# Eight gather slots and eight kept weight chunks in a two-layer encoder with gathered experts

## What is computed

```
h = h + mixer_ab(rmsnorm(h), ...)          # layer 0: stick-breaking attention heads + short gated convolution
h = h + peer(rmsnorm(h), w_q[0], keys[0], u[0], v[0])
h = h + mixer_conformer(rmsnorm(h), ...)   # layer 1: pw1 (1024x2048), GLU, 31-tap conv, layernorm, SiLU, pw2
h = h + peer(rmsnorm(h), w_q[1], keys[1], u[1], v[1])
out = rmsnorm(h)[16:]

peer: q = y @ w_q;  s = q . sub_keys (8 heads, 2 halves, 128 keys)
      top 16 of each half, 16 x 16 sums, top 16 of these -> expert ids, gate = softmax
      act = gate * gelu(u[expert] . y);   out = sum over heads and the 16 of act * v[expert]
```

## Times and profile before

| | |
|---|---|
| median of 3 runs | 1624.63 us (1623.06 to 1624.73) |
| the profiled execution | 1626.37 us, of which the span is 1624.6 us |
| busy share PE / DVE / ACT / POOL | 64% / 69% / 28% / 31% |
| moved by DMA | 649.84 MB, mean 400 GB/s |
| of it the gathers | 528, 553.68 MB |
| of it weights, from SP | 176 chunks of 512 KB |

### The profile page before, as it was taken

The page is one execution under the profiler, slowest core; times in us unless marked ns, Lnnn a source line. Parts: engine busy times, 40 slices in busy tenths (PEclk is TensorE's granted clock), DMA queues, the critical chain, the costliest instruction groups (busy, mean ns, idle before and its releaser), DMA issues.

```text
span 1624.6 us, 19989 instructions
## 1 busy us (share of the span) xinstructions
PE 1046.7 (64%) x6936; PEld 712.2 (44%) x6936; DVE 1113.1 (69%) x3119; ACT 462.3 (28%) x953; POOL 502.6 (31%) x541
## 2 busy tenths in 40 slices
PE   8996876747644476867573477776576444544454
PEld 8995643525411265756451165655364111211111
DVE  3446768675577765987756765897756777777764
ACT  4101544111011235743121134763222111111110
POOL 0012334322233322333313322332323333333330
PEclk9997868868855799888796579887897566666655
DMA  9969999999999999899999999899999999999994
GB/s 371 355 230 380 417 411 408 419 421 417 418 422 421 421 418 417 352 421 407 420 416 421 421 419 417 353 409 394 415 418 405 422 422 422 421 422 422 421 421 194
DMA packets 106164, 649.84 MB, mean 400 GB/s; under 512 B 11728, under 2 KB 15824, under 8 KB 38480
## 3 DMA queue, kind: packets, MB, share of 16 engines
q0 software_dynamic: 76032, 553.68, 82.4%
q1 hardware_dynamic: 26400, 92.81, 14.7%
q10 hardware_dynamic: 3632, 2.08, 0.4%
HBM read 647.48 MB, written 1.05 MB: 399 GB/s over the span
## 4 chain that ended last, share of the span: by engine, by line
DMA 40%; PE 26%; DVE 16%; POOL 5%; ACT 5%; issue 5%; DVEq 2%; POOLq 0%; ACTq 0%
DMA ring<-in_uv_dram,expert 33%; PE ps L668 13%; DMA wring<-in_wall_dram 8%; DVE ring L1197 7%; PE ps L845 7%; POOL ring L391 5%; ACT side L569 2%; PE ps L858 2%; DVE side L1252 2%; PE ps L675 1%; ACT L460 1%; PE ps L833 1%; DVE picked L1189 1%; DVE mix L1213 1%; PE ps L886 1%
## 5 line engine op out<-in xcount | busy, mean ns | idle before, releaser
L1197 DVE CUSTOM_DVE_ANT_0 ring<-ring,ps 128x1024 f32<-128x1024 f32 x528 | 635.2, 1219 | 321.2 <-DMA ring<-in_uv_dram,expert 250.8
L391 POOL DMA_INDIRECT ring<-in_uv_dram,expert x528 | 500.5, 948 | 1086.6 <-PE ps L845 840.0
L845 PE MATMUL ps<-ring,mix 128*32 128x512 f32 x2112 | 365.6, 827 | 311.4 <-DVE mix L1213 311.2
L845 PEld LDWEIGHTS ps<-ring,mix 128*32 128x32 f32 x2112 | 67.4, 134 | 509.7 <-DVE mix L1213 367.8
L668 PE MATMUL ps<-yT,wring 128*128 128x128 f32 (+1 forms) x1472 | 205.6, 301 | 71.8 <-DMA wring<-in_wall_dram 43.7
L642 ACT ACTIVATE gel<-dots 128x4 f32<-128x4 f32 x132 | 27.1, 205 | 739.2 <-DVE dots L1197 738.8
L668 PEld LDWEIGHTS ps<-yT,wring 128*128 128x128 f32 x1472 | 193.6, 207 | 94.6 <-DMA wring<-in_wall_dram 48.1
L858 PE MATMUL ps<-sel,osb 128*128 128x16 f32 x528 | 84.0, 304 | 78.6 <-ACT osb L628 78.6
L858 PEld LDWEIGHTS ps<-sel,osb 128*128 128x128 f32 x528 | 80.6, 241 | 116.7 <-ACT osb L628 116.7
L569 ACT ACTIVATE side<-ident,params 128x128 f32<-128x128 f32 x310 | 96.5, 389 | 16.0 <-PE ps L886 14.8
L833 PE MATMUL ps<-ident,yg 128*128 128x128 f32 x264 | 49.1, 348 | 71.6 <-DVE dots L1197 71.6
(11 more groups left out here) (207 smaller groups left out, 1043.8 us busy)
## 6 DMA issues: line engine op xcount, KB each, us to landing
wring<-in_wall_dram SPq DMA_DIRECT2D x124, 512.0 KB, 12.2
ring<-in_wall_dram SPq DMA_DIRECT2D x52, 512.0 KB, 13.2
ring<-in_uv_dram,expert POOLq DMA_INDIRECT x528, 16.3
out_dram<-fo ACTq DMA_DIRECT2D x16, 64.0 KB, 6.9
hT<-in_xT_dram ACTq DMA_DIRECT2D x1, 576.0 KB, 15.9
hT<-in_xT_dram SPq DMA_DIRECT2D x2, 256.0 KB, 3.3
params<-in_smalls_dram ACTq DMA_DIRECT2D x1, 380.0 KB, 19.2
params<-in_smalls_dram ACTq DMA_DIRECT2D x1, 50.0 KB, 2.8
```

The source lines that it names most:

```text
L391: pool.indirect_dma_start(out=ring[:, i % R, :], out_offset=None, in_=uv, in_offset=bass.IndirectOffsetOnAxis(ap=expert[:, n % 2, k:k + 1] ...
L845: mm = pe.matmul(po[32 * j:32 * j + 32, half, :], mix[:, k, :], ring[:, slot, D + 512 * half:D + 512 * (half + 1)], start=(q == 0), stop=( ...
L1197: nc.vector.tensor_tensor_reduce(out=row, in0=row, in1=yrep, scale=1.0, scalar=0.0, op0=ALU.mult, op1=ALU.add, accum_out=dots[:, k:k + 1]) ...
```

## The change

The ring has 8 slots in place of 12. The freed 32 KB per partition are a tile `kept`, which first holds layer 0's scratch tiles and then the first eight chunks of pw1, loaded once and used in both windows. The 16 early chunk places now fill the whole ring, so each of the first eight gathers waits for chunk inB 2i+1. SP loads the kept chunks ahead of inB 16, and waits ahead of them for the last of layer 0's queries (qA 15) and for the normed tokens (`s_y`). On DVE `weights` now stands ahead of the routing piece in every quarter. ACT runs a Gelu on one element per partition before the Gelus of each step.

```
-R = 12
+R = 8
+KEEP = 8
...
+            if (name, k) == ("inB", 16):
+                for i in range(KEEP):
+                    for w in range(2):
+                        LOADED[JOB["pw1%d" % w, i]] = len(STREAM)
+                    STREAM.append((48 + i, JOB["pw11", i]))
...
             for k in range(count):
-                LOADED[JOB[name % w, k]] = len(STREAM)
-                STREAM.append((row + k, JOB[name % w, k]))
-    FREE = 4
+                if JOB[name % w, k] not in LOADED:
+                    LOADED[JOB[name % w, k]] = len(STREAM)
+                    STREAM.append((row + k, JOB[name % w, k]))
     EARLY = LOADED[JOB["inB", 15]] + 1
-    BUFFER = [(i - EARLY) % (NB + 16) if i < EARLY else (i - EARLY) % NB for i in range(len(STREAM))]
+    BUFFER = [(i - EARLY) % (NB + 2 * R) for i in range(EARLY)] + [NB + 2 * R + i for i in range(KEEP)]
+    BUFFER += [i % NB for i in range(len(STREAM) - len(BUFFER))]
...
+        kept = sb("kept", [P, KEEP * D])
...
-        carve, room = carver(flat[:, 0:8 * D])
+        carve, room = carver(kept)
...
             for i, (row, job) in enumerate(STREAM):
+                if i == EARLY:
+                    evacuated(sp, "qA", 15)
+                    sp.wait_ge(s_y, 1)
...
-                    elif i >= FREE:
-                        pool.wait_ge(s_proj, JOB["inB", 2 * (i - FREE) + 1] + 1)
+                    else:
+                        pool.wait_ge(s_proj, JOB["inB", 2 * i + 1] + 1)
...
+                act.activation(warm[:, :], epsc[:, :], ACT.Gelu)
                 for q in range(4):
...
+                    weights(n, q)
                     if q == 0 and n + 1 < N:
                         route_pairs(n + 1)
...
                     if q == 3 and n + 2 < N:
                         route_best(n + 2)
-                    weights(n, q)
```

More of the change, by code:

```diff
@@ L182, in hybrid_trunk @@
         gel = sb("gel", [P, TOPK])
+        warm = sb("warm", [P, 1])
         coef = sb("coef", [P, TOPK])
@@ L241, in weights_at @@
                 return wring[:, b, :, :]
-            return flat[:, (4 + b) * D:(5 + b) * D].rearrange("p (c n) -> p c n", n=P)
+            t, b = (flat, b - NB) if b < NB + 2 * R else (kept, b - NB - 2 * R)
+            return t[:, b * D:(b + 1) * D].rearrange("p (c n) -> p c n", n=P)
         ps = ctx.enter_context(nc.psum_tensor("ps", [P, 8, 512], f32))
@@ L262, in hybrid_trunk @@
         s_par = sem("s_par")
-        s_w = [sem(f"s_w{b}") for b in range(NB + 16)]
+        s_w = [sem(f"s_w{b}") for b in range(NB + 2 * R + KEEP)]
         s_par2 = sem("s_par2")
```

## The result

The change makes the kernel **8.2% slower**: 1754.47 us (1751.92 to 1766.03, four runs) against 1624.27 us, ratio 1.0816 (95% interval 1.0779 to 1.0853). The prediction said 1661 us, with 1628 to 1695 as its range. The direction was right; 36 us were foreseen and 130 came, well outside the range.

What follows compares the result with a forecast made beforehand. The kernel was taken as DMA-bound at about 422 GB/s, with dips at start, windows and tail. Weights -18, steps without side work +22, start +12, windows +20 sum to +36: about 1661 us, range 1628 to 1695.

Steps and rivals of the forecast that it cites:

- plain steps: Steps without side work or weight loads: 42.4 us against 40.9 with 8 slots, over 14.5 steps, +22 us (0 to +43).
- T: Time from a quarter's last landing to the first reissue of its slots, dot included; 6.0 to 6.8 us without side work.
- S: Time from a quarter's first reissue to the fourth landing, put at 14.6 us.
- The rival with S = 13.0: Shallow queue fills as well as the deep one, so no step without side work loses: 1616 us, chance 0.15.
- The small Gelu and SP's new wait: ACT's one-element Gelu hides in its waits for dots, 0; SP's wait for qA 15 at the start, 0 (+2 uncovered).
- the windows, +20 put: Two convolution windows: slots freed late behind side work cost 10 us each, +20 together (+6 to +40).
- one window quarter (11.0, 7.5 us): In the convolution, slots of quarter 11.0 go out late, so quarter 11.2 ends its dots 7.5 us later.
- two quarters take 30 us, more than T + S: nothing: Quarters with weight loads, 3.77 us a gather: eight slots cost 0 there.
- -18 for fewer weights: Windows: eight pw1 chunks no longer load in either, 9 us saved in each, -18 (-8 to -20).
- the start, +12 put: First quarters: the ninth gather must wait for the first values, and steps 1 to 3 meet this again; +12 (+2 to +18).
- the order: Weights ahead of the routing piece on DVE: gives back 3.1 us in quarter 0 and 3.9 in quarter 1 of a step.
- The rival "the windows don't give back": Every quarter whose values stand behind side work loses as 11.0 does: 1691 us, chance 0.17.

Runs made afterwards that it cites:

- experiment 3: Kernel before with gathers round 8 of its 12 slots and weights ahead of the route's piece, without the change's other parts: 1758.4 us, ratio 1.0784.
- experiment 8: Changed kernel with DVE's front and side pieces ahead of the dots: 1738.9 us; kernel before likewise: 1622.2 us; kernel before, side pieces only: 1621.5 us.
- experiments 1: Kernel before, 12-slot tile kept, with gathers round only 8 of the slots and nothing else changed: 1805.3 us, ratio 1.1050.
- Experiment 4: Changed kernel with pw1's first eight chunks loaded again in each window, the kept ones loaded but not used: 1757.3 us, ratio 1.0777.
- experiment 2: Kernel before, 12 slots, with weights ahead of the route's piece and nothing else: 1640.7 us, ratio 1.0045.
- experiment 9: Half the matmuls of pw1, pw2 and layer 1's query projection left out, all loads kept: changed kernel 1744.7 us, kernel before (12 slots) 1622.3 us.

## Why the prediction was right or wrong

**Right: what bounds plain steps.** T was put at 6.0, 6.4, 6.0, 6.8 and measured at 6.0, 6.0, 6.5, 6.7. S was put at 14.6 and measured at 15.0. Plain steps were +22 us and are +23. The stretch after 1354 runs at 394 GB/s (405 foreseen). In S there was luck. It was taken from an idle queue and one quarter of the convolution (14.7). On the idle queue the first gather lands 5.4 us after its issue and the others follow 4.2, 2.5 and 2.5 us apart; in the loop the first lands after 7.5 us (5.5 foreseen) and the others 2.5 us apart, and both sums are near 15. The rival with S = 13.0 had the spacing of 2.5 right and the first landing wrong, and S = 15.0 refutes it. The Trainium skill's rule for one DMA ("DMA: Bandwidth & Descriptors", section "Anatomy of one DMA") gave an estimated 11.6 us for S; S = 15.0 disagrees with it. The small Gelu and SP's new wait were costed at nothing, and experiment 3 shows no cost of them.

**Wrong: the windows, +20 put, 71 measured.** This is the step that failed most. The law for plain steps, two quarters take at least T + S, was worked out for one window quarter (11.0, 7.5 us) and then replaced by a guess that part comes back. For quarters with weights it was set aside, "two quarters take 30 us, more than T + S: nothing". That is the sentence that failed: over 9.3 to 15.1 the kernel before took 12.1 us a quarter, so 24 for two, and T + S after the change is 10.8 + 16.6 = 27.4 (S is 13 to 18 in most quarters, and up to 23.5 where weight chunks load in between). A quarter takes 13.8. That is 1.65 x 22.5 = 37 us a window. The 10 us lost in pw1 lie in the very quarters that were put at nothing, and of the 7.5 us put on quarters 11.0 to 11.2 some 1 came. What I took for slack, DVE's backlog of up to 9 us behind its landings, was the depth itself: it shrinks with the four slots (dots end 3.4 us after their landings before and 1.9 after in the first window, 5.3 and 2.3 at the start, 1.25 being the least). With a deep ring the side's pieces on DVE run between dots whose data lies ready; with a shallow one they stand behind dots that wait for landings, and landing, dot, piece, PE's side work, values, reissue form one chain (the rows of quarter 9.3 above; experiment 8 takes the piece out of it and wins 15 us, of the windows' 71 some 12). That eight slots cause the loss is shown by experiments 1 and 3; how it divides over the links of this chain is in part argued.

**Wrong: -18 for fewer weights, 0 measured.** Experiment 4 shows it. 4.2 MB fewer are moved in a window, but the window is no longer bound by bytes: DMA runs at 355 and 352 GB/s there, and at 408 and 404 before. Two terms of the sum, one taken as DMA-bound and one as slot-bound, excluded one another, and I added them.

**Wrong: the start, +12 put, +33 measured.** The first third was right: at quarter 1.0 it is +10. Steps 1 to 3 were named and not priced. Over quarters 0.2 to 3.1 T is 10.3 (3.3 us of it from mix to values, where front work stands ahead on PE; 0.35 in plain steps) and S 15.7, 13.0 a quarter against 10.8 before: 2.2 x 12 = 27 of the 33 us, the first quarters' included. The gathers' gating has no part in it: experiment 3 has the old start and loses 34.

**Half right: the order.** It was said to give back 3 to 4 us in two quarters of four, and with 8 slots it does (experiments 1 and 3). That it costs elsewhere was not seen (experiment 2, +7 us with 12 slots): the route's pieces had covered the wait for the Gelu.

The rival "the windows don't give back", at 0.17 and 1691, had the mechanism, and too small a price for the same reason.

**What stays open.** Why the first gather of a quarter takes 7.5 us to land in the loop and 5.4 on an idle queue; and why half of PE's work in pw2 and the query projection is not on the chain (experiment 9 shows that it isn't; PE waits 21 us for ACT's copies of the queries in that window, in place of 5, which makes them only the likeliest cause). PE's clock is not separated either: its mean in the first window fell from 0.88 to 0.81 with the change, and one matmul of the values takes 690 ns there in place of 638. From mix to values it is 5.1 us after the change and 4.7 before, so the clock can be only a small part of the loss, but no run holds it fixed.

## What to carry to other kernels

A ring whose slots come free in groups has a loop time: from a group's landing to its reissue, and from there to the landing of the group that takes its place; divided by the number of groups in the ring it must stay below the transfer time of a group, in every stage, with the waits as they are when the backlog is gone. A consumer's backlog behind landed data is the ring's depth, not spare time. And bytes saved were worth nothing here in a stage that the same change takes off the bandwidth bound.

## What the runs showed of the hardware

A quarter of four gathers (4.2 MB) needs 15.0 us from first issue to last landing with two older gathers still on their way (at 27 of 32 reissues in steps 24 to 31; three at the others), and 14.6 on an idle queue; back to back they take 9.9. The first gather of a quarter lands 7.5 us after its issue in the shallow ring, and 5.4 us on the idle queue. In the stretch in which the queue refills, DMA counts as 0.90 to 0.94 busy and moves 315 to 321 GB/s, so its busy share hides most of the loss (kernel after, step 26):

```profile
1475.50:1478.00 2.50, 0.81 (x10) 0.71 (x6) 1.25 (x3) 0.00 (x0) 1.38 (x2) 1.00 1.00 419
1478.00:1480.50 2.50, 0.00 (x0) 0.00 (x0) 1.27 (x3) 0.00 (x0) 1.89 (x3) 0.60 0.94 321
1480.50:1483.00 2.50, 1.49 (x7) 1.52 (x8) 2.08 (x10) 1.57 (x3) 0.47 (x1) 0.50 0.90 315
1483.00:1485.50 2.50, 2.50 (x15) 0.65 (x17) 2.41 (x11) 2.47 (x5) 0.00 (x0) 0.53 1.02 424
```
